# Two pieces of a projection moved from scan units 6 and 14 to the seam ahead of scan unit 0

## The reference, cut to what matters

```python
h = rmsnorm(x, norm1_w[layer]) * (1.0 + sc1) + sh1
p = h @ w_in[layer]
xl = jax.nn.silu(dwconv_centred(p[..., :XB_CH], ...))          # X and B: conv, 5 taps
cl = jax.nn.silu(dwconv_centred(p[..., OFF_CF:OFF_Z], ...))    # C: conv, 5 taps
y_f = ssd_scan(xs, dtl[:, :, 0], a[0], bf, cf, hf_ctx)         # forward scan
y_b = ssd_scan(xs[:, ::-1], ...)[:, ::-1]                      # backward scan
z = p[..., OFF_Z:OFF_F]                                        # 2048 columns: gate of the scan's output
u = p[..., OFF_F:OFF_GF]                                       # 1024 columns: input of the Fourier branch
```

## Time and profile before

| what | us |
|---|---|
| median of 3 runs | 2525.97 (2525.24 to 2527.53) |
| the profiled execution, its own time | 2525.89 |
| its span, first to last instruction | 2524.6 |
| PE busy in the span | 2448.0 (97%) |
| DVE busy | 1101.5 (44%) |
| ACT busy | 925.2 (37%) |
| conv blocks of the second part | about 1075 to 1275 |
| the seam (pieces 0 and 1, turns 53 to 55) | 1275.6 to 1285.5 |
| scan units 0 to 15 | 1285.5 to 1419 |
| dense part, then router | to about 1595 |
| experts | 1595 to 2515 |

### The profile page before, as it was taken

How to read it: one execution, slowest core, us unless ns; L and a number is a source line. 1 busy time by engine, 2 the same in 40 slices (tenths; PEclk the granted TensorE clock), 3 DMA queues, 4 the chain that set the end, 5 groups by cost and what they waited for, 6 DMA issues and landing times.

```text
span 2524.6 us, 32233 instructions
## 1 busy us (share of the span) xinstructions
PE 2448.0 (97%) x13068; PEld 1669.6 (66%) x13068; DVE 1101.5 (44%) x1700; ACT 925.2 (37%) x1462; POOL 176.1 (7%) x162
## 2 busy tenths in 40 slices
PE   7999899999999999999999999999999999999998
PEld 6888778888887688897977888444444433444433
DVE  5446475554554755468776655321111111111111
ACT  5435364454444454466655642211111111111111
POOL 1000200000002000050600000000000000000000
PEclk9999999999999999999999999999999999999999
DMA  6556665555555765443523346999999999999997
GB/s 256 186 173 210 223 250 186 184 192 188 184 195 208 265 222 184 162 137 122 167 100 101 124 137 242 367 431 432 431 430 432 431 431 432 431 430 432 431 432 332
DMA packets 69328, 688.27 MB, mean 273 GB/s; under 512 B 7938, under 2 KB 8082, under 8 KB 11888
## 3 DMA queue, kind: packets, MB, share of 16 engines
q1 hardware_dynamic: 66224, 675.98, 68.6%
q0 software_dynamic: 3008, 10.95, 1.3%
HBM read 683.76 MB, written 1.05 MB: 271 GB/s over the span
## 4 chain that ended last, share of the span: by engine, by line
PE 67%; DMA 22%; DVE 5%; ACT 4%; issue 2%; POOL 0%; SPq 0%; ACTq 0%; DVEq 0%
PE bank L444 38%; DMA ring<-in_stream 21%; PE bank L2976 12%; PE bank L1911 4%; PE bank L2924 2%; PE bank L482 2%; ACT split_r L399 1%; DVE ring_r L410 1%; DVE work L1969 1%; PE bank L2966 1%; PE bank L763 1%; PE bank L2311 1%; PE bank L1098 1%; PE bank L1297 1%; PE bank L485 1%
## 5 line engine op out<-in xcount | busy, mean ns | idle before, releaser
L410 DVE TENSOR_TENSOR ring_r<-ring,split_r 128x2048 fp32r<-128x2048 f32 (+1 forms) x211 | 476.8, 2284 | 354.1 <-ACT split_r L399 354.0
L444 PE MATMUL bank<-split_r,xT_r 128*128 128x512 f32 (+1 forms) x1760 | 549.4, 390 | 10.3 <-DVE ring_r L410 9.3
L399 ACT CAST split_r<-ring 128x2048 fp32r<-128x2048 f32 (+1 forms) x228 | 429.2, 1905 | 157.3 <-PE bank L444 123.6
L444 PEld LDWEIGHTS bank<-split_r,xT_r 128*128 128x128 f32 x1760 | 331.0, 189 | 79.7 <-issue 13.0
L2976 PE MATMUL bank<-ring,work 128*64 128x512 f32 x1536 | 346.8, 596 | 21.7 <-DMA ring<-in_stream 20.0
L444 PE MATMUL bank<-ring_r,xT_r 128*128 128x512 f32 (+1 forms) x880 | 341.2, 388 | 0.0
L444 PE MATMUL bank<-split_r,work_r 128*128 128x512 f32 x960 | 300.8, 391 | 0.5 <-DVE ring_r L410 0.5
L2976 PEld LDWEIGHTS bank<-ring,work 128*64 128x64 f32 x1536 | 105.4, 137 | 234.3 <-issue 184.6
L2976 PE MATMUL bank<-split,work 128*64 128x512 f32 x1024 | 232.5, 596 | 0.0
L444 PEld LDWEIGHTS bank<-split_r,work_r 128*128 128x128 f32 x960 | 180.2, 188 | 38.0 <-DVE ring_r L410 0.9
L444 PEld LDWEIGHTS bank<-ring_r,xT_r 128*128 128x128 f32 x880 | 166.5, 189 | 32.2
(11 more groups left out here) (402 smaller groups left out, 2900.9 us busy)
## 6 DMA issues: line engine op xcount, KB each, us to landing
ring<-in_stream SPq DMA_DIRECT2D x256, 1024.0 KB, 5.0
ring<-in_stream SPq DMA_DIRECT2D x96, 2048.0 KB, 23.9
split<-in_stream SPq DMA_DIRECT2D x64, 2048.0 KB, 22.2
work<-in_stream SPq DMA_DIRECT2D x32, 2048.0 KB, 23.7
row<-in_rows POOLq DMA_DIRECT2D x6, 512.0 KB, 4.3
ring<-in_stream SPq DMA_DIRECT2D x4, 560.0 KB, 4.7
work<-in_conv POOLq DMA_DIRECT2D x2, 768.0 KB, 5.7
x<-in_x SPq DMA_DIRECT2D x1, 1024.0 KB, 10.2
```

Of the source, the lines that this page charges most:

```text
L399: act.copy(hi, self.part(half, self.ring)).then_inc(*up("half_hi", half.h))
L410: dve.tensor_tensor(self.part(half, self.ring_lo), self.part(half, self.ring), hi.bitcast(F32), ALU.subtract).then_inc(*up("half_lo", half.h))
L444: mm = self.nc.tensor.matmul(out, a[x][a_at], w[y][w_at], start=start and n == 0, stop=stop and n == 2)
```

## The change

The list of pieces gives four pieces (0 to 3) to unit 0, that is to the seam, and takes one from unit 6 and one from unit 14. The seam makes pieces 2 and 3 as well, one ahead of the turn of block 55 and one behind it. Everything that follows from the list moves along: the pieces of units 1 to 5 have numbers higher by two, those of units 6 to 13 by one, and each engine splits a half in the unit before the first piece that needs it.

```diff
@@ -1781,7 +1781,7 @@
         self.units = [(d, m, g) for g in range(NG2) for d, m in ((0, 0), (1, 1), (0, 1), (1, 0))]
         self.pieces, p = [], 0
         for u in range(16):
-            n = 1 if u % 2 else 2
+            n = 4 if u == 0 else 1 if u % 2 or u in (6, 14) else 2
             self.pieces.append(range(p, p + n))
             p += n
         assert p == 24
@@ -2157,7 +2157,9 @@
         self.pe_piece(0)
         self.pe_conv_turn(54)
         self.pe_piece(1)
+        self.pe_piece(2)
         self.pe_conv_turn(55)
+        self.pe_piece(3)
```

## The result

The median of 13 runs is 2533.21 us (2527.03 to 2536.65), beside 2526.94 us (2524.36 to 2531.25) for the kernel before in as many runs. The ratio is 1.0021, with an interval from 1.0013 to 1.0029: some 5.3 us slower by the ratio and 6.3 us by the two medians, where the forecast was 4.2 us. The median is 1.2 us above the upper end of the range. The three runs that the forecast started from had a median of 2525.97; 13 runs put it 1.0 us higher.

What follows compares the result with a forecast made beforehand. PE was taken to bound seam and scan, with DVE level at unit 1; pieces 0, seam -0.7, DVE's split +3.4 and clock +1.5 gave +4.2 us, from 2525.97 to 2530.2 us, range 2527.5 to 2532.0.

Steps and rivals of the forecast that it cites:

- What bounds the kernel: Seam and scan: PE bounds the time, but at unit 1's state(1) DVE, handing over xw(1), is level with it.
- The two pieces: Two pieces of 2.7 us each come to the seam and leave units 6 and 14: 5.4 - 5.4 = 0.
- The seam's gain: Seam: piece 3 covers ACT's copy in the wait for the last turn, gain 0.7 us (0.5 to 0.9).
- Unit 1's loss: Unit 0 must split a half; DVE's part delays xw(1) and so state(1) of unit 1: loss 3.4 us.
- The clock: Behind unit 1's stall of 3.6 us PE runs at half speed for a stretch: +1.5 us (0 to 2.1).
- rival of a long slow stretch: Clock stays low through unit 1 and unit 2's pieces: +5.8 us, 2531.8 us, from a price of 2.35 us; chance 0.13.
- a clock that holds: Rival: same stall in unit 1 but no slow stretch behind it, +2.7 us, 2528.7 us; chance 0.25.
- `xw(1)` did not come in time: Rival: DVE's split costs nothing as xw(1) comes in time, only the gain stays, -0.7 us, 2525.3 us; chance 0.06.
- units 6 and 14 did shrink: Rival: units 6 and 14 don't shrink, 2.7 us more for each, 2532.9 or 2535.6 us; chance 0.06.
- Everything behind the scan follows unchanged but later: Dense part, router and experts: only shifted later by the scan's delay, nothing added to the sum.
- a shift that changes between unit 15 and the experts: Sign of being wrong: from unit 15 on all should be shifted by one constant.
- The start of the sum: Whole kernel: +4.2 us put on 2525.97 us, the median of the runs shown, giving 2530.2 us.

Runs made afterwards that it cites:

- e2: Kernel before, pieces unmoved, only the split of the third half (ACT and DVE) moved from unit 1 to unit 0: ratio 1.0022.
- e4: Changed kernel with the third half split in the seam, on ACT between the turns of blocks 54 and 55, on DVE after its projections: ratio 1.0006, median 2527.66 us.
- e6: Kernel of e4 with piece 2 put ahead of piece 1 in the seam: ratio 0.9996.
- e3: Changed kernel with 28 matmuls without use on PE ahead of state(1) of unit 1: ratio 1.0020, median 2531.71 us.
- e8: Kernel before with 28 matmuls without use in each of PE's two idle times of 4.66 us in the mixers: ratio 0.9984, median 2523.49 us.
- e1: Changed kernel again, no edit, against the kernel before: ratio 1.0022, median 2532.23 us.
- e11: Changed kernel with matmuls without use in the mixers' two idle times alone, unit 1's idle time left: ratio 1.0018, median 2531.34 us.
- e5: Kernel before again with its own profile, as a control: ratio 1.0002.

## Why the prediction was wrong

**What bounds the kernel: right.** The stage is PE's, and `state(1)` was level with DVE. e2 shows it: the split moved to this point on ACT and DVE, with no piece moved, costs the whole 3.4 us.

**The two pieces: right.** Units 2 to 14 take 107.34 instead of 112.82 us, 5.48 less for two pieces (5.4 forecast).

**The seam's gain: right.** From conv to unit 0 it is 4.88 us more for 5.4 us of pieces, so 0.5 to 0.6 us are gained; together with units 0 and 1 in e4, where nothing stalls, 0.68 us (0.7 forecast). The new pieces fill neither wait for the taps, and e6, which lets piece 2 pass piece 1, gets those 1.7 us.

**Unit 1's loss: right.** 3.61 us of wait instead of 0.22: 3.39 forecast and 3.39 measured; e2 has 3.38. With the full clock (e3) the stage is 2.68 us longer, where the sum without the clock gave 2.7.

**The clock: right in kind, too small in size; this term of the sum failed.** The step put +1.5 us, the smaller of two prices, since the idle time was shorter. Four profiles show 1.6, 1.6, 2.5 and 2.7, about 2.1 in the mean and 2.7 in the changed kernel's own. Two things were wrong in it. Both prices left out the first slow matmul; with it they are about 1.8 and 2.4 us (e8), and the larger one already meets the condition of 2.35 us that the prediction set for its rival of a long slow stretch. And the price isn't set by how long the idle time was but by how much PE work lies in the slow stretch: behind the same 3.6 us of idle time, some 3.4 us of slow work cost 1.6 us in e1 and in e2, some 5.2 us cost 2.5 in e11, and almost 6 cost 2.7 in the changed kernel, each time about half. The larger of the two prices should have been the value and not the end. The rival of the long slow stretch is met by two of the four profiles. The other rivals fall: a clock that holds is seen in none of the unfilled stalls, `xw(1)` did not come in time, and units 6 and 14 did shrink.

**"Everything behind the scan follows unchanged but later": wrong for these runs.** The sum put nothing for these parts. Dense part and router are 1.46 us longer in the changed kernel's profile, the experts 1.15; a shift that changes between unit 15 and the experts was one of the prediction's own signs of being wrong. e5 shows that the kernel before alone can vary by 2.6 us in the experts; the router's part is the open question above, and the mean clocks put the loss outside the scan at about 1 us.

**The start of the sum and the width of the range: wrong.** The step that carried the forecast from +4.2 us to 2530.2 us used the median of three runs. Single runs of the kernel before go from 2524.36 to 2531.25 in 13 runs, and the range held nothing for a median of three that is 1 us low. Of the 3.0 us between 2530.2 and 2533.2, 1.0 is this and 2.0 are the sum's, 6.3 instead of 4.2 us by the medians; against the ratio's 5.3 us the sum missed 1.1. The long slow stretch's +5.8 us on 2526.94 gives 2532.7, and with 1 us of scatter a range to about 2533.7 would have held the result.

The prediction gave 0.76 of the chance to a change of no more than 0.2%; the measured ratio of 1.0021 lies just beyond that line, its interval on both sides of it.

## What to carry to other kernels

When filler work is moved forward, follow what prepares it, not only the filler: here two pieces cost nothing, and the half that had to be split one unit earlier stood in DVE's queue ahead of the one result that PE waited for. Put such a step where its engines stand still anyway (e4), and put the filler ahead of the wait that it is meant to fill, not behind it (e6). An idle time of TensorE such as those of 3.6 and 4.66 us here has a second price behind it, and cheap matmuls in it, without use and shorter than the wait, take that away: 28 in each of two places were worth 3.7 us here (e8), more than the 2.6 us of the reordered seam. In unit 1 the same remedy restored the stage (e3), but what it is worth in the whole time the runs don't fix.

## What the runs showed of the hardware

The price behind an idle time of PE is not fixed for a kernel. The same stall of 3.6 us cost 1.6 to 2.7 us in four profiles, and over 23 runs of the changed kernel the mean granted clock went from 0.992 to 0.996, the time from 2536.65 to 2527.03 us. A few stretches at half speed, each some us long, go with most of the scatter of this kernel: the 32 runs of the kernel before reach from 2522.57 to 2531.07 us, the 13 of them with a mean clock of 0.996 only from 2525.50 to 2527.30, and with the mixers filled, the kernel before has mean clocks of 0.997 to 0.999 and a median 3.7 us lower. "TensorE: Matmul & The Clock Gate" of the Trainium skill says, in part 1 ("The HAM clock gate"), that the moment at which the speed rises at a kernel's start varies from run to run. For slow stretches in the middle of a kernel the profiles of the changed kernel and of e1 show the same, with the slow stretch up to 1309.2 in one, and in two pieces, partly under the wait, in the other.

Also unexpected: a low clock can hide in a wait. In e1 it fell already ahead of the stall, the products of unit 1 ran at half speed, and the wait for `xw(1)` looked 1.5 us shorter (2.12 instead of 3.61 us) while `state(1)` started no later. Who reads the wait alone would take it for a gain.

The clock also fell where PE hardly stood still. In the router of the changed kernel's profile the only idle time of PE from 1540 to 1562 us is one of 0.73 us, and behind 16 products of 32 columns the matmuls of 512 columns take 0.63 us again, until 1565:

```profile
1559.21 0.66 PE L2440 MATMUL bank<-consts,work 128*128 128x128 f32 x4 [0.73 <-DVE work L2594]
1559.81 2.08 PE L2736 MATMUL bank<-work,mod_T 128*128 128x32 f32 x16
...
1563.14 0.63 PE L444 MATMUL bank<-ring_r,work_r 128*128 128x512 f32 x1
...
1565.37 0.40 PE L444 MATMUL bank<-ring_r,work_r 128*128 128x512 f32 x1
```

So a list of long idle times doesn't name every place where half speed can come. The kernel before has the same products there and, in its three profiles, the full clock.
